# The down projection of a feed-forward block as seven quarter products in two phases

## The reference, cut to what matters

```python
D_MODEL, SEQ, D_FF, CONV_W = 1024, 512, 2816, 3
def conv_ffn(h, w_up, conv_w, conv_b, w_down):
    up = h @ w_up                                   # 512 x 1024 @ 1024 x 5632
    upc = conv(up, conv_w) + conv_b                 # 3 taps along the sequence
    gate, val = upc[..., :D_FF], upc[..., D_FF:]
    return (jax.nn.silu(gate) * val) @ w_down       # 512 x 2816 @ 2816 x 1024
...
h = h + conv_ffn(rms_norm(h, norm_ffn[l]), ffn_w_up[l], ...)
```

## Time and profile before

| what | value |
|---|---|
| median of 3 runs | 691.51 us (690.8 to 693.09) |
| profiled execution, span from first to last instruction | 687.5 us |
| TensorE busy in the span | 678.7 us (99%) |
| VectorE, ScalarE, GpSimd busy | 416.6, 317.6 and 142.3 us |
| granted TensorE clock | 1.00 in all of the span |
| stretch of the down projection | from 564.3 to 684.2 us |

### The profile page before, as it was taken

How to read it: one execution, slowest core, us unless ns; L and a number is a source line. 1 busy time by engine, 2 the same in 40 slices (tenths; PEclk the granted TensorE clock), 3 DMA queues, 4 the chain that set the end, 5 groups by cost and what they waited for, 6 DMA issues and landing times.

```text
span 687.5 us, 11261 instructions
## 1 busy us (share of the span) xinstructions
PE 678.7 (99%) x4105; PEld 562.4 (82%) x4105; DVE 416.6 (61%) x699; ACT 317.6 (46%) x558; POOL 142.3 (21%) x140
## 2 busy tenths in 40 slices
PE   8999999999999999999999999999999999999998
PEld 7978877877788788888988888888888888888886
DVE  4999997678765674649575545555545654333332
ACT  5738563867744564745443334333333532223310
POOL 4999995032221101510000000000000000000000
PEclk9999999999999999999999999999999999999999
DMA  8747554565210411111233132231323323233203
GB/s 259 227 139 125 164 143 130 167 195 208 68 57 1 153 51 73 62 62 41 83 123 122 61 122 85 98 121 62 122 63 120 101 82 123 67 116 109 74 0 123
DMA packets 63002, 73.99 MB, mean 108 GB/s; under 512 B 20873, under 2 KB 47796, under 8 KB 62836
## 3 DMA queue, kind: packets, MB, share of 16 engines
q1 hardware_dynamic: 59700, 67.17, 31.0%
q10 hardware_dynamic: 3264, 6.31, 2.8%
HBM read 68.08 MB, written 5.78 MB: 107 GB/s over the span
## 4 chain that ended last, share of the span: by engine, by line
PE 86%; POOL 4%; DMA 3%; ACT 3%; DVE 2%; SPq 1%; issue 1%; DVEq 0%; POOLq 0%; ACTq 0%
PE pb L517 25%; PE pb L519 25%; PE pb L518 25%; PE pb L1830 7%; PE pb L1833 4%; POOL F L706 2%; DMA raw<-in_w_in 1%; ACT F L913 1%; DMA F<-F 1%; DMA raw<-in_x_wkv 1%; DVE F L1300 1%; SPq L620 1%; ACT xs L913 0%; DVE wring L503 0%; POOL F L819 0%
## 5 line engine op out<-in xcount | busy, mean ns | idle before, releaser
L500 DVE TENSOR_TENSOR wring<-raw,wring 128x1024 fp32r<-128x1024 f32 x95 | 124.5, 1312 | 67.7 <-ACT wring L489 67.4
L517 PE MATMUL pb<-xs,wring 128*128 128x512 f32 (+1 forms) x448 | 165.3, 369 | 0.1
L519 PE MATMUL pb<-xs,wring 128*128 128x512 f32 (+1 forms) x448 | 164.2, 366 | 0.0
L518 PE MATMUL pb<-xs,wring 128*128 128x512 f32 (+1 forms) x448 | 164.1, 366 | 0.0
L489 ACT ACTIVATE wring<-raw 128x1024 fp32r<-128x1024 f32 x100 | 105.0, 1054 | 81.7 <-PE pb L519 70.9
L1306 DVE SCALAR_TENSOR_TENSOR F<-pb,ccol,F 128x511 f32<-128x511 f32 x88 | 66.0, 750 | 103.4 <-ACT F L913 97.5
L517 PEld LDWEIGHTS pb<-xs,wring 128*128 128x128 f32 x448 | 84.5, 189 | 14.4 <-issue 0.6
L517 PE MATMUL pb<-wring,bs 128*128 128x512 f32 x240 | 95.8, 399 | 0.1
L519 PEld LDWEIGHTS pb<-xs,wring 128*128 128x128 f32 x448 | 84.4, 189 | 14.0
L518 PEld LDWEIGHTS pb<-xs,wring 128*128 128x128 f32 x448 | 84.5, 189 | 13.3
L519 PE MATMUL pb<-wring,bs 128*128 128x512 f32 x240 | 93.6, 390 | 0.0
(11 more groups left out here) (148 smaller groups left out, 788.0 us busy)
## 6 DMA issues: line engine op xcount, KB each, us to landing
raw<-in_ffn_w_up SPq DMA_DIRECT2D x22, 1024.0 KB, 5.1
raw<-in_ffn_w_down SPq DMA_DIRECT2D x11, 1024.0 KB, 4.9
F<-in_x SPq DMA_DIRECT2D x8, 512.0 KB, 5.7
raw<-in_w_in ACTq DMA_DIRECT2D x4, 1024.0 KB, 5.9
raw<-in_w_out SPq DMA_DIRECT2D x4, 1024.0 KB, 4.8
raw<-in_w_in SPq DMA_DIRECT2D x3, 1024.0 KB, 7.2
raw<-in_x_wkv ACTq DMA_DIRECT2D x2, 1024.0 KB, 5.5
raw<-in_x_wkv SPq DMA_DIRECT2D x2, 1024.0 KB, 5.6
```

What stands on the lines that cost most here:

```text
L500: ins = nc.vector.tensor_tensor(w_unit(u, 1), raw_unit(u), w_unit(u, 0).bitcast(f32), ALU.subtract)
L517: nc.tensor.matmul(ps, lh, rh, start=first, stop=False)
L518: nc.tensor.matmul(ps, lh, rl_, start=False, stop=False)
L519: return nc.tensor.matmul(ps, ll, rh, start=False, stop=last)
```

## The change

The product is regrouped. Two blocks of 128 hidden columns make a pair, 11 pairs in all. The hidden values of a pair are cut into quarters by token half and block (A11, A12 for the first 256 tokens, A21, A22 for the last), and the weights by block and column half (B11, B12, B21, B22). Four quarters of the output are made of seven products instead of eight:

- P7 = (A11-A21)(B22-B12), P5 = (A21+A22)(B12-B11), P3 = (A12-S2) B22, P6 = S2 (B22-(B12-B11)) with S2 = A21+A22-A11, in the first phase (`e`, in the code x = 0 to 3);
- P1 = A11 B11, P2 = A12 B21, P4 = A22 (B22-(B12-B11)-B21) in the second phase (`d`, x = 0 to 2).

Each product of a pair is 256 tokens by 512 columns: two banks, three matmuls each. The first phase runs over all pairs and fills eight banks; these are added into the quarters of the residual that need them; the second phase runs over the pairs once more and fills six. The last two pairs of a phase are done bank by bank. Weights are loaded a second time for the second phase (the left 512 columns alone).

The sums are made before the splits: per pair four sums of hidden quarters (128x256, `hidden_sums`) and two of the weights (128x512, `down_sums`: B12-B11 and B22-B12) on GpSimd, and the third of the weights (`second_sum`: B22-(B12-B11)) on VectorE; in the second phase one more weight sum per pair (`down_last`) on GpSimd. Split weights have two slots of a pair each (ring halves), split hidden blocks three, raw weights three. The diff, cut to its core, in the order tables, SP, GpSimd (`pool`), ScalarE (`act`), VectorE (`dve`), TensorE (`pe`):

```diff
+NP = FT // 2
+E_BANK = ((4, 5), (6, 7), (0, 1), (2, 3))
+        def w_pieces(g):
+            r = down_raw(g)
+            if g < NP:
+                return [(0, 2, r[:, 512:1536]), (2, 1, r[:, 1536:2048]), (3, 1, t2_store(g))]
+            return [(0, 2, r[:, 0:1024]), (2, 1, r[:, 1024:1536])]
+        def h_pieces(g):
+            if g < NP:
+                return [(0, 1, h_quarter(g, 0, 1)), (1, 3, h_sums(g).rearrange("p a n -> p (a n)"))]
+            at = (g - NP) * 2 * T
+            return [(0, 1, h_quarter(g - NP, 0, 0)), (1, 2, hff_flat[:, at + T:at + 2 * T])]
...
-            with sync.Fori(0, FT // 4) as i:
-                load_chunk(sync, U_DOWN // 2, i)
-                load_chunk(sync, U_DOWN // 2 + 1, i)
+            for g in range(2 * NP):
...
+                if g >= 3:
+                    sync.wait_ge(dw_lo, pieces_before(g - 2))
...
+            def hidden_sums(i):
+                pool.wait_ge(hff_ready, 2 * i + 2)
+                a11, a21, a12, a22 = (h_quarter(i, j, half) for j in range(2) for half in range(2))
+                s1, s4, s2 = (h_sums(i)[:, n, :] for n in range(3))
+                link(add(s1, a21, a22))
+                sub(a21, a11, a21)
+                link(sub(s2, s1, a11))
+                sub(s4, a12, s2).then_inc(sum_ready, 1)
+            def down_sums(g):
...
+                pool.wait_ge(down_in[g % 3], 16 * (g // 3 + 1))
+                link(sub(b21, b12, b11))
+                sub(b12, b22, b12).then_inc(t_ready, 1)
+            for i in range(NP - 1):
+                hidden_sums(i)
+            down_sums(0)
+            down_sums(1)
+            hidden_sums(NP - 1)
+            for g in range(2, NP):
+                down_sums(g)
+            pool.wait_ge(t2_ready, NP)
+            for g in range(NP, 2 * NP):
+                down_last(g)
...
+            def down_hi(g):
+                for n, (x, w, src) in enumerate(w_pieces(g)):
...
+                    elif n != 1:
+                        act.wait_ge(t2_ready if n == 2 else t_ready, g + 1)
+                    if g >= 2:
+                        slot_used(act, g - 2, x + w - 1)
+                    A_(w_block(g, 0)[:, x * 512:(x + w) * 512], src, ACT.Copy).then_inc(dw_hi, 1)
...
+            def second_sum(g):
+                r = down_raw(g)
+                dve.wait_ge(t_ready, g + 1)
...
+                tt(t2_store(g), r[:, 1536:2048], r[:, 1024:1536], ALU.subtract).then_inc(t2_ready, 1)
+            def down_lo(g):
+                for n, (x, w, src) in enumerate(w_pieces(g)):
+                    at = slice(x * 512, (x + w) * 512)
+                    dve.wait_ge(dw_hi, pieces_before(g) + n + 1)
+                    tt(w_block(g, 1)[:, at], src, w_block(g, 0)[:, at].bitcast(f32), ALU.subtract).then_inc(dw_lo, 1)
+            def hidden_lo(g):
+                dve.wait_ge(h_hi, g + 1)
+                for x, w, src in h_pieces(g):
...
+            up_round(FT // 2 - 1, last=True)
+            for g in range(2, NP):
+                second_sum(g)
+                hidden_lo(g)
+                down_lo(g)
+            product_out(0, 0)
+            product_out(0, 1)
+            hidden_lo(NP)
...
+            for g in range(NP + 1, 2 * NP):
+                hidden_lo(g)
+                down_lo(g)
+                if g < NP + 3:
+                    product_out(3, g - NP - 1)
...
+            def down_phase(pre, g0, products):
+                for g in range(g0, g0 + NP - 2):
+                    for x in range(products):
+                        for t in range(2):
+                            p = fill(pe, f"{pre}{x}{t}") if g == g0 else pb[E_BANK[x][t]]
+                            ins = down_product(g, x, t, p, g == g0, False)
+                        ins.then_inc(down_used, 1)
+                for x in range(products):
+                    for t in range(2):
+                        down_product(g0 + NP - 2, x, t, pb[E_BANK[x][t]], False, False)
+                        filled(down_product(g0 + NP - 1, x, t, pb[E_BANK[x][t]], False, True), f"{pre}{x}{t}")
+            down_phase("e", 0, 4)
+            down_phase("d", NP, 3)
```

More of the change, by code:

```diff
@@ L238, in layer @@
         bank_free = [sem(f"bank_free{i}") for i in range(8)]
-        act_hi, act_lo = sem("act_hi"), sem("act_lo")
+        act_hi = sem("act_hi")
+        sum_ready, t_ready, down_used = sem("sum_ready"), sem("t_ready"), sem("down_used")
+        down_in = [sem(f"down_in{i}") for i in range(3)]
+        left_ready = sem("left_ready")
+        t2_ready = sem("t2_ready")
+        h_hi, h_lo, dw_hi, dw_lo = sem("h_hi"), sem("h_lo"), sem("dw_hi"), sem("dw_lo")
         sq_done = sem("sq_done")
@@ L329, in plan @@
                 use(j % 4, f"f{j}")
-            for b in range(8):
-                use(b, f"d{b}")
+            for x in range(4):
+                for t in range(2):
+                    use(E_BANK[x][t], f"e{x}{t}")
+            for x in range(3):
+                for t in range(2):
+                    use(E_BANK[x][t], f"d{x}{t}")
         plan()
@@ L506, in split_lo @@
             ins.then_inc(lo_done, 1)
-        def split_next(eng, split, i, j):
-            if isinstance(i, int) and i == FT // 2 - 1:
-                split(eng, U_DOWN + j)
-            else:
-                split(eng, U_UP + 4 + j, i)
         def mm3(ps, lh, ll, rh, rl_, first, last):
@@ L1251, in _, with up_round @@
             x_hi("x3", 3)
-            def up_round(i, first=False, split=None):
+            def up_round(i, first=False, last=False):
                 for j in range(4):
@@ L1259, in up_round @@
                     A_(cv[:, j, :], p[:, :], ACT.Identity, scale=tap, bias=shift).then_inc(conv_ready, 1)
-                    split_next(act, split_hi, i, j)
+                    if not last:
+                        split_hi(act, U_UP + 4 + j, i)
+                    elif j in (0, 2):
+                        down_hi(j // 2)
                     if j < 2:
@@ L1783, in _, with up_round @@
             before_up = n_step[0]
-            def up_round(i):
+            def up_round(i, last=False):
                 for j in range(4):
@@ L1793, in up_round @@
                     drained(stt(o[:, 2:], p[:, 0:T - 2], tap[0], o[:, 2:], ALU.mult, ALU.add), f"f{j}")
-                    split_next(dve, split_lo, i, j)
+                    if not last:
+                        split_lo(dve, U_UP + 4 + j, i)
+                    elif j in (1, 3):
+                        down_lo(j // 2)
+                    else:
+                        second_sum(j // 2)
                     if j >= 2:
@@ new lines, in to_output, with product_out @@
+            def to_output(name, i, j, t, op=ALU.add):
+                o = hres[:, 2 * i + t, j * 512:(j + 1) * 512]
+                return tt(o, o, read(dve, name)[:, :], op)
+            def product_out(x, t):
+                quarters = (((1, 0), (1, 1)), ((0, 1), (1, 1)), ((0, 1),), ((0, 1), (1, 0), (1, 1)))[x]
+                if x > 0:
+                    after_drain(dve, f"e{x - 1}{t}")
+                for i, j in quarters:
+                    ins = to_output(f"e{x}{t}", i, j, t)
+                drained(ins, f"e{x}{t}")
@@ L1809, in _ @@
             with dve.Fori(0, FT // 2 - 1) as i:
                 up_round(i)
-            for n in range(4):
-                down_lo(n)
-            up_round(FT // 2 - 1)
-            with dve.Fori(0, FT // 4 - 1) as r:
-                for n in range(4, 8):
-                    split_lo(dve, U_DOWN + n, r)
-                    down_lo(n, r)
-            for n in range(FT // 4 * 4, FT):
-                split_lo(dve, U_DOWN + n)
-                down_lo(n)
-            for b in D_ORDER:
-                t, half = b // 2, b % 2
-                o = hres[:, t, half * 512:(half + 1) * 512]
-                tt(o, o, read(dve, f"d{b}")[:, :], ALU.add).then_inc(res_ready, 1)
+            hidden_lo(0)
@@ new lines, in _ @@
+            for t in range(2):
+                after_drain(dve, f"e3{t}")
+                for i, j in ((0, 1), (1, 1), (0, 0), (1, 0)):
+                    ins = to_output(f"d0{t}", i, j, t)
+                    if j == 1:
+                        ins.then_inc(res_ready, 1)
+                ins.then_inc(left_ready, 1)
+            for t in range(2):
+                dve.wait_ge(left_ready, t + 1)
+                to_output(f"d1{t}", 0, 0, t).then_inc(res_ready, 1)
+            for t in range(2):
+                to_output(f"d2{t}", 1, 0, t, ALU.subtract).then_inc(res_ready, 1)
```

160 lines of the change are left out of this document (97 added, 63 removed).

## The result

| | before | after |
|---|---|---|
| median, lowest to highest, runs | 690.44 us, 689.38 to 693.09, 20 | 693.50 us, 691.49 to 695.32, 20 |
| ratio of after to before, 95% interval | | 1.0044 [1.0034, 1.0053] |
| profiled execution: its own time, span | not given, 687.5 us | 694.20 us, 692.4 us |
| matmuls of the down projection | 528 | 462 |
| first to last matmul of it | 119.45 us | 123.50 us |

A forecast was written before the change was run, and what follows sets the result against it. TensorE's number of matmuls was taken to bound the down projection. 76.0 + 46.1 + 0.6 = 122.7 against 119.7 (15.0 saved, 18.0 given back) is +3.0: 694.5 us from 691.5, range 680 to 701, the forecast's own 691 to 700.

The forecast's parts named there:

- The gain, 66 x 0.2267 = 15.0: Down projection on TensorE: 462 matmuls for 528 at an unchanged 0.2267 us each, 15.0 us saved.
- The two engines shut each other out: VectorE and GpSimd take turns on two-SBUF-input instructions; a first-phase pair costs 6.3 us against TensorE's 5.44; chance 0.50.
- The start: First phase, pair 2: VectorE stands from 5.5 to 11.7 for GpSimd's sums; TensorE waits 8 us, until about 19.
- First weights of pair 10 at 65.8: First phase: the shared VectorE and GpSimd work ends at 65.8 us after the first down matmul.
- the load is no matter: Start of the first phase: weight loads take 4.9 us but are issued a pair or more ahead.
- From pair 5 on waits some 0.86 per pair: First phase: TensorE, at 5.44 us per pair, waits for shared work of 6.3 us per pair.
- The end of the first phase, 76.0: After pair 10's first weights 45 matmuls, 10.2 us, are left; the phase ends at 76.0 instead of 59.9.
- the second rival: TensorE's clock falls in its waits: 0 to 24 matmuls at half clock, 0 to 5.4 us, 2.7 taken: 697; chance 0.22.
- The second phase, 46.1 + 0.6: Second phase: 44.9 us plus 1.2 of waits, and 0.6 for VectorE's additions from PSUM slowed beside GpSimd.
- the three instructions of 1.03: Trace row read as PSUM additions beside GpSimd, 1.03 us each against 0.69 alone; up to 0.43 more each.
- The bounds: On the total: GpSimd sums at 1.05 give 2.5 less, at 1.29 4.2 more; additions up to 1.4 more.
- the first rival: No contention that matters between VectorE and GpSimd: waits of 4.0 at pair 2 and 0.6 at the end, 681 us; chance 0.20.

The follow-up runs named there:

- e2: Changed kernel with GpSimd's two weight sums per first-phase pair replaced by constant writes of 128x1024, order and signals kept: 680.23 us, ratio 0.9863 to the kernel before.
- e4: Changed kernel with all weight sums on VectorE, the second phase's too, and only the hidden sums on GpSimd: 683.64 us, ratio 0.9930 to the kernel before.
- e6: Changed kernel: GpSimd does two weight sums for pairs 0 to 2 early; VectorE all three of pairs 3 to 10 and pair 10's hidden sums: 682.59 us.
- e3: Changed kernel with the third weight sum of a pair moved from VectorE to GpSimd too: 698.42 us, ratio 1.0131 to the kernel before.
- e7: Changed kernel with VectorE doing a pair's hidden splits before its third weight sum: 694.16 us, ratio 1.0057 to the kernel before.
- e8: e6 with only the first phase's last pair bank by bank, and the second phase's first splits before the additions: 680.14 us, ratio 0.9867 to the kernel before.
- e9: Kernel before, with two probes of unused 128x512 subtractions on VectorE and GpSimd in the down projection: 688.87 us.
- e10: Kernel before, with five probes: VectorE runs of subtractions meeting one GpSimd sum, varying signal place, waits, signals and widths: 706.04 us, one run.

## Why the prediction was right

- **The gain, 66 x 0.2267 = 15.0.** Held: 462 matmuls, and pairs that don't wait take 5.44 and 4.08 us.
- **The two engines shut each other out.** Held: e2 takes the reading away and 12.3 us go; e4 and e6 take the sums off GpSimd and 8.9 and 10.4 go; e3 puts more on it and 5.9 come. The 1.15 for a sum, from the earlier trace rows, was 1.11 in e3.
- **The start.** "TensorE gets pair 2 at about 19, a wait of 8 us": 18.96 and 8.1, by the chain that was named. VectorE stood from 5.7 to 11.5, where 5.5 to 11.7 had been forecast.
- **First weights of pair 10 at 65.8.** 66.15. But a part of the working under it failed: "the load is no matter ... issued a pair or more ahead". A slot of raw weights comes free behind the splits of three pairs earlier, and here those are late. Pair 5's load is issued when pair 2's last split ends, as SP's timeline after shows, and GpSimd's sum starts 5.0 us later, when it has landed (590.28 in GpSimd's timeline above).

```profile
585.27 0.37 SPq L758 DMA_DIRECT2D F<-in_ffn_w_down  x1
```

- **"From pair 5 on waits some 0.86 per pair."** This was false in place and about right in sum: 1.3 and 3.0 at pairs 5 and 8, none at 6, 7 and 9, where 5 x 0.86 = 4.3 had been forecast. The wait in the midst of the last two pairs cost 2.0, where some 4 had been named. GpSimd waits 7 us for every third pair's load, and VectorE runs freely meanwhile; then both sums are late and VectorE waits 2.6 us for them:

```profile
596.10 1.77 DVE L1421 TENSOR_TENSOR F<-F 128x512 f32<-128x512 f32 x1 [2.56 <-POOL F L802]
```

  What VectorE saved by sums that did not meet it, some 4 x 1.1 us, it lost again in two such waits (5.1 us): that the total came out near the forecast is partly luck.
- **The end of the first phase, 76.0.** 78.08. The 45 matmuls behind 66.15 took 11.9 us instead of 10.2: eight ran at 0.43. This is the second rival, the clock, at a part of its size (0 to 5.4, 2.7 taken): a matmul at 0.43 costs 0.20 more, not the 0.2267 of the rival. The granted clock was 0.50, the lower of its two levels (1.2 GHz), in two stretches: one began in the midst of the wait of 8 us and lasted to 587.7, one held from 632.5 to 635.5, behind the waits at pairs 8 and 10. The windows, the last column but two is the clock:

```profile
581.00:584.20 3.20, 0.01 (x1) 0.04 (x1) 3.20 (x3) 0.66 (x2) 1.89 (x2) 0.50 0.00 0
584.20:587.70 3.50, 3.50 (x8) 2.77 (x9) 3.50 (x6) 1.67 (x3) 0.00 (x0) 0.50 0.30 85
611.00:623.00 12.00, 9.26 (x41) 7.32 (x39) 9.45 (x8) 4.89 (x8) 10.63 (x6) 1.00 0.42 161
632.50:635.50 3.00, 3.00 (x8) 2.34 (x7) 1.73 (x3) 0.00 (x0) 2.32 (x2) 0.50 0.50 166
```

  The first stretch cost nothing, as forecast: TensorE waited for VectorE again at pair 5 anyway.
- **The second phase, 46.1 + 0.6.** 45.4 to its last matmul's start: 0.7 at the last pair (0.6 forecast) and nothing else. The additions from PSUM did not lose to GpSimd's sums. Three took 1.87 us with a sum of GpSimd inside them, and five took 3.06 where GpSimd was idle:

```profile
638.17 3.06 DVE L1421 TENSOR_TENSOR F<-F,pb 128x512 f32<-128x512 f32 x5
...
646.17 1.87 DVE L1421 TENSOR_TENSOR F<-F,pb 128x512 f32<-128x512 f32 x3
```

```profile
646.73 1.30 POOL L802 TENSOR_TENSOR F<-F 128x512 f32<-128x512 f32 x1 [9.02 <-DMA F<-in_ffn_w_down]
```

  That is 0.60 each for VectorE either way, and 1.30 for GpSimd's sum. So the rule of the Trainium skill (SBUF — State Buffer, "Who interferes with whom") that the prediction weighed held here. The prediction misread: the three instructions of 1.03 are no such additions but products (line 1462) that read both inputs in steps of 8 elements, and all four of their kind stand beside GpSimd, so they can't show what GpSimd costs them. Other instructions of the same trace with one input in PSUM read it in sequence, and beside GpSimd two of 256 columns took 0.75 us, one 0.33 after the other, which is what the prediction took for 256 columns without GpSimd. VectorE's timeline of the kernel before, then GpSimd's:

```profile
58.13 0.75 DVE L1300 TENSOR_TENSOR F<-pb,F 128x256 f32<-128x256 f32 x2
```

```profile
58.14 2.08 POOL L706 TENSOR_TENSOR F<-pw,F 128x512 f32<-128x512 f32 x2
```

  The 0.6 us that the sum took for this were not lost.

In the trace the stage is 4.05 us longer where 3.0 were forecast. The 1.0 between them is 0.35 (pair 10) and 1.7 (clock) less 1.05 (the second phase). The stage also starts 0.95 later, so the two spans differ by 4.9: the trace of after is one of its longer executions (694.20 against a median of 693.50). The 4.0 us that the prediction kept outside the span compare a median of three runs with the span of one; in the later runs of the kernel before, where both are known of one execution, 1.7 to 1.9 lie outside. That the medians differ by 3.1, as forecast, is partly luck. The bounds don't come out either: 16 sums at 1.05 give 1.6 less and at 1.29 with no issue hidden 3.4 more, not 2.5 and 4.2. And a range of 680 to 701 takes in the first rival, so a time inside it says little; the waits and e2 carry the argument. The mechanism and its largest terms were right.

## What to carry to other kernels

A helper engine is free only if it does not stop the engine that it helps: count a GpSimd sum of two SBUF tensors as time of VectorE too, and compare it with what VectorE would need (here 1.15 for 0.60). When the helped engine has a long queue up to one late point, add up all the work up to that point: a wait taken away earlier (e7) comes back later. And when one engine gets faster, look at where it stands in the order when the next late result comes (e6, e8): the two changes of order in e8 were worth 2 us.

## What was not expected of the hardware

- GpSimd's sum was now and then kept out over several VectorE instructions in a row, not for one. The longest took 5.43 us, for work of 1.15; it ended 1.16 us after VectorE's run, which ended at 658.80:

```profile
654.53 5.43 POOL L802 TENSOR_TENSOR raw<-F,raw 128x512 f32<-128x512 f32 x1 [2.64 <-DMA raw<-in_ffn_w_down]
```

  e9 and e10 show turns in most runs and one such stand (2.87 us); what decides is open.
- The half clock did not follow the length of a single wait. After, 2.0 us lost at pair 10, with 3.0 lost at pair 8 ahead of it, brought eight slow matmuls, which began 0.8 us after the wait; in e4, 2.4 lost at the same place with none since pair 2 brought none: the 45 matmuls took 10.3 us, and the clock was 1.00 around it. But in e4 the 2.5 lost at pair 2, behind unbroken work, did bring six slow matmuls. The windows of e4, about the wait at pair 10 and behind the wait at pair 2:

```profile
617.50:625.00 7.50, 5.29 (x23) 4.05 (x23) 7.40 (x13) 2.50 (x5) 0.00 (x0) 1.00 0.35 128
577.30:580.70 3.40, 3.37 (x8) 2.72 (x9) 3.40 (x7) 1.08 (x2) 0.00 (x0) 0.50 0.27 77
```

  The Trainium skill (TensorE: Matmul & The Clock Gate, "What's actually happening") says that an idle array drops to 1.2 GHz; these rows agree, with 0.43 us for a matmul at a granted clock of 0.50. Two waits of nearly the same length in one kernel differ in what followed, so neither the length of a wait nor an earlier wait decides by itself; what does was not tried.
